# A hybrid decoder layer on one core: the output stage's first group begun on tiles 1 and 2, its tables loaded in the tail of the stage before

## The reference, cut to what matters

```python
def block(xb):
    q = (xb @ wq).reshape(PEER_BLOCK, PEER_HEADS, 2, PEER_HALF)
    s = jnp.einsum('thpd,hpkd->thpk', q, subkeys).astype(jnp.float32)
    s_top, i_top = lax.top_k(s, PEER_TOPK)
    ...
    g_s, g_i = lax.top_k(cand, PEER_TOPK)
    e = jnp.take_along_axis(cand_idx, g_i, axis=-1)
    g = jax.nn.softmax(g_s, axis=-1).astype(xb.dtype)
    act = jax.nn.gelu(jnp.einsum('thed,td->the', u[e], xb))
    return jnp.einsum('the,thed->td', g * act, v[e])
```

## Time and profile before

| what | us |
|---|---|
| median of 3 runs (2139.04 to 2143.4) | 2142.75 |
| profiled execution, its own time | 2144.45 |
| its span, first to last instruction | 2142.8 |
| PE busy | 1983.4 (93%) |
| DVE busy | 1585.5 (74%) |
| ACT busy | 849.7 (40%) |
| POOL busy | 586.1 (27%) |

### The profile page before, as it was taken

One profiled execution on the slowest core, in us unless ns is written; L12 is line 12 of the kernel. 1 busy time (PEld: TensorE's weight loads), 2 busy tenths in 40 slices (PEclk: granted clock), 3 DMA queues, 4 the chain that ended last, 5 costly groups with the idle time before them and its releaser, 6 DMA issues.

```text
span 2142.8 us, 32281 instructions
## 1 busy us (share of the span) xinstructions
PE 1983.4 (93%) x10400; PEld 1615.9 (75%) x10400; DVE 1585.5 (74%) x3165; ACT 849.7 (40%) x1723; POOL 586.1 (27%) x590
## 2 busy tenths in 40 slices
PE   8998989678889899999999899998969999999997
PEld 6774656443446568899999899998967888888886
DVE  4564257657323446999989989998958899989988
ACT  1233032123202321244777577667823333333332
POOL 1002231233100000003211222225625554544452
PEclk9999889879899999999999999999989999999999
DMA  6343335789830421358888899899999999999994
GB/s 216 78 116 107 109 117 194 263 331 320 295 134 3 160 77 59 126 166 287 274 270 251 287 300 311 259 317 374 398 347 388 384 393 405 395 389 387 387 386 161
DMA packets 240962, 547.46 MB, mean 255 GB/s; under 512 B 22382, under 2 KB 123567, under 8 KB 239418
## 3 DMA queue, kind: packets, MB, share of 16 engines
q1 hardware_dynamic: 180490, 337.69, 45.8%
q0 software_dynamic: 60336, 208.10, 26.5%
HBM read 485.08 MB, written 60.02 MB: 254 GB/s over the span
## 4 chain that ended last, share of the span: by engine, by line
PE 40%; DVE 12%; issue 4%; DMA 4%; ACT 2%; SPq 1%; POOL 0%; DVEq 0%; ACTq 0%; POOLq 0%
PE psum L3074 23%; PE psum L2796 9%; PE psum L2316 5%; DVE u_gather L2690 3%; PE psum L2812 2%; DVE uL L2442 2%; DMA u_raw<-in_uT 2%; DVE hT L2722 1%; DMA u_gather<-in_u_rows,gather_ids 1%; DMA S<-activation_table 1%; PE psum L2307 1%; SPq L2568 1%; DVE eq L2226 1%; DVE eq L2223 1%; ACT hT L2657 0%
## 5 line engine op out<-in xcount | busy, mean ns | idle before, releaser
L2432 POOL DMA_INDIRECT u_gather<-in_u_rows,gather_ids x160 | 194.5, 1216 | 811.7 <-DVE dots L2690 476.6
L2796 PE MATMUL psum<-hH,uH 128*128 128x384 f32 x1024 | 356.1, 348 | 6.2 <-DVE uL L2442 6.2
L2796 PE MATMUL psum<-hL,uH 128*128 128x384 f32 x1024 | 347.2, 339 | 0.0
L2796 PE MATMUL psum<-hH,uL 128*128 128x384 f32 x1024 | 346.8, 339 | 0.0
L3074 PE MATMUL psum<-vH,wH 128*128 128x512 f32 x768 | 301.1, 392 | 20.4 <-DVE wL L3003 20.4
L2911 POOL DMA_INDIRECT Gtile<-in_v_rows,idx_now x160 | 231.9, 1450 | 256.7 <-DVE y_sample L3010 157.7
L3074 PE MATMUL psum<-vL,wH 128*128 128x512 f32 x768 | 300.5, 391 | 0.0
L3074 PE MATMUL psum<-vH,wL 128*128 128x512 f32 x768 | 300.3, 391 | 0.0
L2690 DVE CUSTOM_DVE_ANT_0 u_gather<-u_gather,h 128x1024 f32<-128x1024 f32 x160 | 195.5, 1222 | 15.5 <-DMA u_gather<-in_u_rows,gather_ids 11.0
L2796 PEld LDWEIGHTS psum<-hH,uH 128*128 128x128 f32 x1024 | 196.0, 191 | 8.3 <-DVE uL L2442 8.1
L2796 PEld LDWEIGHTS psum<-hL,uH 128*128 128x128 f32 x1024 | 196.1, 192 | 0.0
(11 more groups left out here) (540 smaller groups left out, 3270.2 us busy)
## 6 DMA issues: line engine op xcount, KB each, us to landing
u_raw<-in_uT SPq DMA_DIRECT2D x128, 512.0 KB
S<-in_v_rows SPq DMA_DIRECT2D x64, 512.0 KB
Gtile<-in_v_rows SPq DMA_DIRECT2D x64, 512.0 KB
activation_table<-acts SPq DMA_DIRECT2D x128, 192.0 KB
gate_table<-Gtile SPq DMA_DIRECT2D x48, 512.0 KB
S<-gate_table SPq DMA_DIRECT2D x16, 768.0 KB
S<-activation_table SPq DMA_DIRECT2D x16, 768.0 KB
G_rest<-gate_table SPq DMA_DIRECT2D x16, 768.0 KB
```

Of the source, the lines that this page charges most:

```text
L2432: c.nc.gpsimd.indirect_dma_start(c.ug[:, k % RG], None, c.A["u_rows"].rearrange("j i d -> (j i) d"), bass.IndirectOffsetOnAxis(ap=c.ids[:, ...
L2796: ins = nc.tensor.matmul(column[n % 4][:, 0:ND], w[:, n % RU, d], x[:, d], start=m == 0, stop=m == len(parts) - 1)
```

## The change

In the tail SyncE's `flush(i)` issues, after each of the columns 122, 123 and 124, one of the three gate stores left of block 10. Behind these and column 125 it loads, one each, the gates of blocks 0 to 7 for group 0 (tiles 1 and 2, 512 KB), the activations of group 0 (768 KB) and two rows of v. The four stores of the last block are issued by ScalarE after column 125. What remains for the end of SyncE's block is the last third of the gates, 256 KB. Group 0 in the output stage works on 256 columns for its four items (wf, wH, wL, TensorE's tiles 1 and 2), then on 128 columns for its four items (tile 3). Its last item is split in the group itself. The matmuls of tile 3 signal that an item is done (`v_mm`); gelu of the dots moves behind all copies of the group.

```diff
@@ stage_activate, SyncE @@
-                steps(columns, *[nothing] * 7, unit, nothing, nothing)
-                sp.wait_ge(res_ready, STILE)
-                for j in range(2):
-                    sp.dma_start(c.v_raw[j], A["v_rows"][j]).then_inc(c.v_in[j], 16)
-                for n in range(NUNIT - GATES_BEHIND, NUNIT):
-                    if n % BUNIT < STORES:
-                        store_gates(n // BUNIT - 1, n % BUNIT)
-                for i in range(STORES):
-                    store_gates(NTB - 1, i)
+                def flush(i):
+                    left = [n for n in range(NUNIT - GATES_BEHIND, NUNIT) if n % BUNIT < STORES]
+                    if i < len(left):
+                        store_gates(left[i] // BUNIT - 1, left[i] % BUNIT)
+                    if i == 0:
+                        sp.wait_ge(res_ready, STILE)
+                        for q in range(2):
+                            sp.wait_ge(G_stored[q], 16 * STORES * (EARLY_BLOCKS // 2))
+                        sp.dma_start(c.G_group[0][:, 0:EARLY_BLOCKS * GS * TB], A["gates"][0][:, 0:EARLY_BLOCKS * GS * TB]
+                                     ).then_inc(c.G_in[0], 16)
+                    elif i == 1:
+                        for q in range(RA):
+                            sp.wait_ge(a_stored[q], 16 * len(range(q, GS, RA)))
+                        sp.dma_start(c.a_group[0], A["acts"][0:GS].rearrange("j p t -> p j t")).then_inc(c.G_in[0], 16)
+                    elif i < 4:
+                        sp.dma_start(c.v_raw[i - 2], A["v_rows"][i - 2]).then_inc(c.v_in[i - 2], 16)
+
+                steps(columns, *[nothing] * 7, unit, nothing, flush)
...
-                sp.dma_start(c.G_group[0], A["gates"][0]).then_inc(c.G_in[0], 16)
-                sp.dma_start(c.a_group[0], A["acts"][0:GS].rearrange("j p t -> p j t")).then_inc(c.G_in[0], 16)
+                sp.dma_start(c.G_group[0][:, EARLY_BLOCKS * GS * TB:], A["gates"][0][:, EARLY_BLOCKS * GS * TB:]
+                             ).then_inc(c.G_late, 16)
@@ stage_activate, ScalarE's flush @@
+                    if i == AHEAD:
+                        act.wait_ge(g_ev, NUNIT)
+                        for part in range(STORES):
+                            act.dma_start(*gate_block(NTB - 1, part)).then_inc(G_stored[(NTB - 1) % 2], 16)
@@ stage_experts, VectorE @@
+                def first_group():
...
+                    dve.wait_ge(G_in[0], 32)
+                    for j in range(GS):
+                        if j >= 2:
+                            dve.wait_ge(wa_done, j - 1)
+                        V.tensor_tensor(blocks(wf[:, j % 2, 0:ED]), blocks(a[0][:, j, 0:ED]),
+                                        gates[:, 0:EARLY_BLOCKS, j], ALU.mult).then_inc(wa_full, 1)
+                        if j:
+                            first_split(j - 1)
+                    first_split(GS - 1)
+                    dve.wait_ge(c.G_late, 16)
+                    dve.wait_ge(wa_done, GS)
+                    for j in range(GS):
+                        if j >= 2:
+                            dve.wait_ge(w_done, j - 1 + 2 * GS)
+                        V.tensor_tensor(blocks(wf[:, j % 2, ED:ND]), blocks(a[0][:, j, ED:ND]),
+                                        gates[:, EARLY_BLOCKS:NTB, j], ALU.mult).then_inc(w_full, 1)
+                        if j:
+                            late_split(j - 1)
+                    late_split(GS - 1)
...
                     for j in range(GS):
-                        product(r, b, j)
-                        if j:
+                        if not first:
+                            product(r, b, j)
+                        if j and not first:
                             split(r, b, j - 1)
-                        elif not first:
+                        elif not j and not first and not (r is None and b == 1):
                             split(r, b - 1, GS - 1)
@@ stage_experts, TensorE @@
+                    if r is None and b == 0:
+                        for j in range(GS):
+                            pe.wait_ge(wa_done, j + 1)
+                            pe.wait_ge(v_split, j + 1 + GS)
+                            for t in range(STILE - 2):
+                                products(j, j, t)
+                        for j in range(GS):
+                            pe.wait_ge(w_done, j + 1 + 2 * GS)
+                            products(j, j, STILE - 2).then_inc(v_mm, 1)
                         return
```

More of the change, by code:

```diff
@@ L2546, in nothing, with gate_block @@
             return None
+        def gate_block(blk, i):
+            part = slice(i * (NG // STORES), (i + 1) * (NG // STORES))
+            return (A["gates"][part, :, blk * (GS * TB):(blk + 1) * (GS * TB)].rearrange("g p n -> p g n"),
+                    G[:, blk % 2].rearrange("p (g j) t -> p g (j t)", j=GS)[:, part])
         with nc.Block() as block:
@@ L2566, in store_gates @@
                         sp.wait_ge(g_ev, (blk + 1) * BUNIT)
[L2567 to L2570, removed]
+                    sp.dma_start(*gate_block(blk, i)).then_inc(G_stored[blk % 2], 16)
                 def unit(p, st, i):
@@ L2946, in _ @@
             def _(act):
+                def first_group():
+                    for j in range(GS):
+                        act.wait_ge(v_in[j], 16)
+                        act.wait_ge(v_mm, j + 1)
+                        nc.scalar.activation(vH[:, j], v[j], ACT.Copy).then_inc(v_hi, 1)
+                        act.wait_ge(wa_full, j + 1)
+                        nc.scalar.activation(wH[:, j, 0:ED], wf[:, j % 2, 0:ED], ACT.Copy).then_inc(wa_hi, 1)
+                    for j in range(GS):
+                        act.wait_ge(w_full, j + 1)
+                        nc.scalar.activation(wH[:, j, ED:ND], wf[:, j % 2, ED:ND], ACT.Copy).then_inc(w_hi, 1)
+                    nc.scalar.activation(gact[:], c.dot[:], ACT.Gelu_apprx_tanh).then_inc(gelu_done, 1)
                 def body(r, b):
+                    if r is None and b == 0:
+                        first_group()
+                        return
                     g = at(r, 2, b)
@@ L3011, in add, with first_group, first_split, late_split @@
                                            ALU.add).then_inc(done, 1)
+                def first_group():
+                    blocks = lambda ap: ap.rearrange("p (b t) -> p b t", t=TB)
+                    gates = c.G_group[0].rearrange("p (b j t) -> p b j t", b=NTB, j=GS)
+                    dve.wait_ge(G_in[0], 32)
[17 more added lines that the diff above has]
+                    late_split(GS - 1)
+                def first_split(j):
+                    dve.wait_ge(v_hi, j + 1)
+                    V.tensor_tensor(vL[:, j], v[j], vH[:, j].bitcast(F32), ALU.subtract).then_inc(v_split, 1)
+                    dve.wait_ge(wa_hi, j + 1)
+                    V.tensor_tensor(wL[:, j, 0:ED], wf[:, j % 2, 0:ED], wH[:, j, 0:ED].bitcast(F32),
+                                    ALU.subtract).then_inc(wa_done, 1)
+                def late_split(j):
+                    dve.wait_ge(w_hi, j + 1)
+                    V.tensor_tensor(wL[:, j, ED:ND], wf[:, j % 2, ED:ND], wH[:, j, ED:ND].bitcast(F32),
+                                    ALU.subtract).then_inc(w_done, 1)
                 def body(r, b):
@@ L3015, in body @@
                     first = r is None and b == 0
+                    if first:
+                        first_group()
                     for j in range(GS):
-                        product(r, b, j)
-                        if j:
+                        if not first:
+                            product(r, b, j)
+                        if j and not first:
                             split(r, b, j - 1)
-                        elif not first:
+                        elif not j and not first and not (r is None and b == 1):
                             split(r, b - 1, GS - 1)
```

8 lines of the change are left out of this document (4 added, 4 removed).

## The result

The change made the kernel slower: 2149.47 us median (2145.61 to 2151.08, 7 runs) against 2140.98 for the kernel before (2137.52 to 2143.4, 7 runs), ratio 1.0036 with a 95% interval of 1.0024 to 1.0048. Forecast were 2137.3 and a range of 2131 to 2145: the sign is wrong and the time outside. Measured once more beside the experiments the ratio was 1.0028 (1.0007 to 1.0048). The profiled execution took 2147.06 us, its span 2145.4.

The account below looks back on a forecast made before the run. TensorE bounds from 1700 us; around the stage border it waits while DMA is nearly full. Barrier 0 and start -5.5 on the profiled 2144.45 give 2138.95, less 1.7 to the runs' median: 2137.3 us, range 2131 to 2145.

Parts of the forecast that it names:

- DMA is full near the gap, so early loads aren't free: Around the border of the two stages: DMA share near 1.0 even in TensorE's gap, so no free DMA time there.
- Last column 2 to 4 us later: Tail of the columns: u loads 123 to 127 find up to 3.9 MB more ahead, delaying the last column 2 to 4 us.
- VectorE's 3.85 us of idle time as a cover: Tail, at 1561 us: VectorE's 3.85 us idle, waiting for ScalarE, was taken to cover part of the u loads' delay.
- The bound of 10.5 us: Tail: upper bound on the last column's delay, 3.9 MB at 375 GB/s; the lower bound was 0.
- Barrier unmoved at 1589.5: Block end before the output stage, counted from as b: stays at 1589.5 us, bounds 1586 and 1596.
- rival A: No change, the bytes decide: barrier moves to 1592.9 (+3.4), DMA's 5.0 gain remains, -1.6 us, 2141.2; chance 0.27.
- Rival B: Slower: u loads and gathers suffer 10.5 us, ScalarE's queue becomes the exit, barrier 1609.5, +14.5 us, 2157.3; chance 0.13.
- VectorE's work after the barrier: Start of output stage: item 0's wL at b+2.9, product 4 at b+19.7, item 4 at b+24.2, item 7 at b+37.3.
- the second old wait, for item 7: Output stage, fourth row of group 1: TensorE's second wait, ended at b+43.4 before, was to go.
- The slow clock at 2.0 us: TensorE behind its wait for item 4: the same 2.0 us charged for a slow clock as behind the old wait.
- Gain of the start 5.5 us: Start of output stage: TensorE's order gives 7.0 us, DMA allows 5.0; 5.5 taken.

Follow-up runs that it names:

- x7: The change with group 0 whole and its four early loads behind the last u load, block 10's gate stores still early; ratio to the kernel before 1.0000.
- x4: The change with SyncE's early transfers (three gate stores, early gates, activations, two v rows) moved behind the last u load; ratio to the kernel before 1.0002.
- x10: x9 with the three gate stores behind columns 125, 126 and 127 in place of 122, 123 and 124; 2135.42 us, ratio to the kernel before 0.9969.
- x2: The change's transfers alone, group 0 computed whole as in the kernel before; ratio to the kernel before 1.0014.
- x5: The change with the first addition of group 1 placed behind item 4's split; ratio to the kernel before 1.0009.
- x1: The kernel before with only block 11's four gate stores moved to ScalarE behind column 125's eviction; ratio to the kernel before 1.0007.
- x8: x4 with the addition behind item 4's split as in x5; ratio to the kernel before 0.9996.
- x9: x7's transfers with x5's two-part group 0 and order of additions; ratio to the kernel before 0.9993.
- x6: x4 with group 0 computed whole as in the kernel before; ratio to the kernel before 0.9991.

## Why the prediction was wrong

**DMA is full near the gap, so early loads aren't free.** Right, and the clue was used on the wrong side. I weighed bytes before the barrier, as if whoever needs them would find them equally late. The transfers were not equal: the u loads of columns 123 to 127, issued before only 4.2 to 11.8 us ahead of their use, stand behind whatever SyncE issued earlier.

**Last column 2 to 4 us later: the step that failed.** It was 12 us (12.3, and 15.3 for the second traces). I counted VectorE's 3.85 us of idle time as a cover. The rows say that this very wait was the lever: VectorE waits there for ScalarE's exponential, which stands behind uH of column 125, and column 124's uL stands behind that wait. Before, the exponential had waited for TensorE, for the eviction of column 122; in the change it waited for the u load of column 125, and so did column 124. ScalarE before:

```profile
1558.67 0.49 ACT L2618 ACTIVATE acts<-psum 128x384 f32<-128x384 f32 x1 [3.52 <-PE psum L2796]
...
1560.97 0.23 ACT L2622 ACTIVATE res_sample<-res_sample 128x32 f32<-128x32 f32 x1
```

VectorE's wait grew from 3.85 to 12.83 us (16.47 in the second trace, 7.52 in x7, but 4.74 in x4 and 2.56 in x10, where u 125 goes out with nothing new ahead of it). Column 124's own late load explains little of TensorE's 12 us: 0.2 in the first trace, 3.3 in the second (from the end of its uH). That the transfers' place costs the 12 us is shown by x2 and x4; that it does so through the exponential is read from the traces, and no run moved the exponential. The bound of 10.5 us that I kept was exceeded too, by 1.8 to 4.8; DMA stood nearly idle for 4 us (19 GB/s), which is of that size.

**Barrier unmoved at 1589.5: wrong.** Counted from the first column it came after 683.3 us (685.0 in the second trace) in place of 677.3 and 675.0: 6 to 10 us later, by late columns and then only 2.6 us to the barrier in place of 8.9. That it reads 1593.0 in the trace, beside rival A's 1592.9, is chance: this trace began its columns 2.5 us earlier than that of before. Rival B comes nearest. Its first half, that the columns suffer the whole backlog of 10.5 us, came true; its second, ScalarE's queue as the exit, did not in the change. Its four stores took 4.74 us, not 9.7, and held nobody for long; DMA moved 249 GB/s from 1582 to 1588. In x4, with DMA at 381 GB/s, they took 11.79.

**VectorE's work after the barrier: right in sum, wrong in a wait.** First matmul at b+3.0 (2.9 forecast), product 4 at b+20.2 (19.7), the second old wait, for item 7, gone. But item 4 came at b+29.4, not 24.2, and TensorE reached item 7 at b+44.3 in place of 38.4. The 4.5 us from product 4 to item 4's wL held no wait for the gathered row. They were taken from a trace in which it was there after 5.9 us, and by taking the split of item 3 out from between I brought the addition 2 us nearer to the gather without asking whether the row would be there. x5 takes most of the wait away by order alone.

**The slow clock at 2.0 us: about right.** Behind item 4's wait the first item took TensorE 6.6 us in place of 4.1, 2.5 lost (before, behind item 7's wait, 5.8: 1.8 lost). It was paid once more, in the tail behind the 12 us, which the sum didn't hold.

**Gain of the start 5.5 us: 0.9 measured.** TensorE did start 5.3 us earlier behind the barrier (b+2.9 in place of 8.3) and lost it again at item 4. With the whole group it was 4.8 more in x2.

Four stores on another queue changed the time by nothing that can be measured (x1: 1.0007, 0.9993 to 1.0022). The rule of the Trainium skill weighed under rival A (DMA: Bandwidth & Descriptors, section on issuing engines not being separate DMA queues) agrees with that.

The two delays less what came back make 5.1 and 9.1 us in the two pairs of traces (sums 1223.1 against 1218.0, 1224.3 against 1215.2), which brackets the 6.2 and 8.5 us of the medians. What stays open is how much of it each of the two holds. x4 takes away the tail's part and is level with before. x5 takes away item 4's part alone and isn't told from before either. Both together (x8) gain less than their sum.

## What to carry to other kernels

A transfer that nobody awaits yet, put into a queue ahead of transfers that are awaited just in time, can cost those its full length and more (12 us here for 3.9 MB); place it behind the last of them, and then look at who waits behind its own stores. When a wait before shows idle time, find out what stands behind that wait on the same engine, and what the awaited instruction itself stands behind, before calling it cover. When work is taken out from between a gather's issue and its use, ask whether the row is there yet.

## What the runs showed of the hardware

A gather of 512 KB was there within 5.9 us of its issue in the kernel before, after 7.8 and 8.2 us in x7 and x2, with group 2's tables issued behind it in all three, and after 8.5 to 9.6 us in eight traces with these 1.6 MB issued on another queue some 5 us before. Four gate stores took ScalarE 4.6 to 4.8 us to issue in the change, x2 and x5, where DMA was less busy (249 GB/s in the change), 8.3 to 8.6 in x1, x7 and x9, and 11.0 to 11.8 in x4, x6, x8 and x10 (381 GB/s in x4). The first column shifts by up to 13.7 us between the traces, more than the effect that was sought; the three stretches repeat within 1.6 us in two traces of the same kernel, and within 4.0 us in kernels that differ only elsewhere.
